# Input projection of a hybrid encoder layer: activations fetched six tiles ahead, inverse roots as powers on GpSimd, first weights in two halves

## The reference, cut to what matters

```python
def rmsnorm(x, w):
    xf = x.astype(jnp.float32)
    y = xf * lax.rsqrt(jnp.mean(xf * xf, axis=-1, keepdims=True) + EPS)
    return (y * w.astype(jnp.float32)).astype(x.dtype)

def hybrid_layer(x, ...):
    xn = rmsnorm(x, norm_mix_w)
    proj = jnp.einsum('btd,de->bte', xn, w_in)
    # q, k, v, forget gate of the attention heads; q/k/v, gates, z of the delta-rule heads
    ...
    h = x + jnp.einsum('bte,ed->btd', mix, w_o)
    # a second norm, up-projection, causal conv, SiLU gate, down-projection, final norm
```

## Time and profile before

| | us |
|---|---|
| median of three runs (4260.08 to 4277.38) | 4275.02 |
| the profiled execution | 4281.21 |
| its span | 4279.7 |
| TensorE busy in it | 3964.6 (93%) |
| VectorE, ScalarE, GpSimd busy | 1663.3, 1283.9, 367.2 |
| piece 0, from its first row product (20.85) to the first of piece 1 (171.10) | 150.25 |

### The profile page before, as it was taken

One profiled execution on the slowest core, in us unless ns is written; L12 is line 12 of the kernel. 1 busy time (PEld: TensorE's weight loads), 2 busy tenths in 40 slices (PEclk: granted clock), 3 DMA queues, 4 the chain that ended last, 5 costly groups with the idle time before them and its releaser, 6 DMA issues. The chain is left out here.

```text
span 4279.7 us, 56482 instructions
## 1 busy us (share of the span) xinstructions
PE 3964.6 (93%) x21471; PEld 3380.8 (79%) x21471; DVE 1663.3 (39%) x3428; ACT 1283.9 (30%) x2333; POOL 367.2 (9%) x346
## 2 busy tenths in 40 slices
PE   5799999799999999989997997999999999899996
PEld 4799999677777777768885446999999999678775
DVE  2100177555445455433331333444444444331222
ACT  6311222233333333321100332333333333231122
POOL 2000000111112111111100000000000000010222
PEclk8899999899999999997777998999999999999999
DMA  2222122411222111042232331111111111342221
GB/s 91 73 68 66 57 69 72 96 33 29 55 42 55 41 36 35 17 134 72 82 104 92 103 100 50 53 43 45 43 52 45 43 43 43 103 125 73 83 83 55
DMA packets 318288, 278.71 MB, mean 65 GB/s; under 512 B 128530, under 2 KB 267394, under 8 KB 318039
## 3 DMA queue, kind: packets, MB, share of 16 engines
q1 hardware_dynamic: 297999, 247.47, 19.8%
q0 software_dynamic: 4896, 17.83, 1.1%
q10 hardware_dynamic: 15228, 11.10, 0.9%
HBM read 190.70 MB, written 85.65 MB: 65 GB/s over the span
## 5 line engine op out<-in xcount | busy, mean ns | idle before, releaser
L2185 PE MATMUL bank<-hn_hi,up_w_parts 128*128 128x436 f32 (+1 forms) x3520 | 981.5, 360 | 10.2 <-DVE up_w_parts L2260 10.2
L2185 PEld LDWEIGHTS bank<-hn_hi,up_w_parts 128*128 128x128 f32 x3520 | 662.1, 188 | 41.9 <-issue 10.3
L2185 PE MATMUL bank<-hn_lo,up_w_parts 128*128 128x436 f32 (+1 forms) x1760 | 632.8, 360 | 0.0
L2185 PEld LDWEIGHTS bank<-hn_lo,up_w_parts 128*128 128x128 f32 x1760 | 331.4, 188 | 19.1
L301 PE MATMUL bank<-proj_wh,proj_xh 128*128 128x256 f32 (+1 forms) x1088 | 318.6, 293 | 2.0 <-DVE proj_wl L467 2.0
L301 PE MATMUL bank<-proj_wl,proj_xh 128*128 128x256 f32 (+1 forms) x1088 | 314.5, 289 | 0.0
L301 PE MATMUL bank<-proj_wh,proj_xl 128*128 128x256 f32 (+1 forms) x1088 | 314.1, 289 | 0.0
L2231 ACT COPY up_raw<-bank 128x436 f32<-128x436 f32 (+1 forms) x220 | 110.3, 502 | 642.2 <-PE bank L2185 612.1
L1365 PE MATMUL bank<-heads_p_pT,heads_p_v 128*65 128x512 f32 (+3 forms) x640 | 287.1, 530 | 10.3 <-issue 10.1
L2434 PE MATMUL bank<-down_w_hi,down_g_hi 128*128 (+1 forms) x748 | 238.1, 400 | 50.2 <-DVE down_g_lo L2529 42.8
L2529 DVE TENSOR_TENSOR down_g_lo<-down_g_raw,down_g_hi 128x256 fp32r<-128x256 f32 (+1 forms) x198 | 111.0, 561 | 389.2 <-ACT down_g_hi L2494 389.2
(11 more groups left out here) (390 smaller groups left out, 6977.1 us busy)
## 6 DMA issues: line engine op xcount, KB each, us to landing
up_w<-in_w_up_dram SPq DMA_DIRECT2D x44, 512.0 KB, 4.8
down_g_raw<-scratch_g SPq DMA_DIRECT2D x88, 256.0 KB, 2.6
scratch_g<-up_acc SPq DMA_DIRECT2D x88, 218.0 KB, 2.0
heads_s_k<-in_cache_fox_k_dram SPq DMA_DIRECT2D x8, 2048.0 KB, 9.4
heads_s_v<-in_cache_fox_v_dram SPq DMA_DIRECT2D x8, 2048.0 KB, 8.1
heads_d_qkvT<-scratch_gch SPq DMA_DIRECT2D x17, 768.0 KB
down_y<-in_w_down_dram SPq DMA_DIRECT2D x22, 512.0 KB, 3.6
scratch_gch<-proj_work SPq DMA_DIRECT2D x48, 218.0 KB, 1.9
```

The source lines that it names most:

```text
L2185: mm = pe.matmul(bank[:, pair(n) + e, 0:width], w_parts[:, a, part, e, k, :], x[:, k, cols], start=(k == 0 and m == 0), stop=(k == KD - 1 ...
```

## The change

- **Fetches of x** go six tiles ahead (`AHEAD`) into two new names, `raw_h` and `raw_l`, which lie on the same memory as `xh` and `xl` in places that are not filled yet: tiles 0 to 7 in a row of `xl` that belongs to later tokens, tiles 8 to 16 in the place in `xh` that the tile itself will fill, as 8 runs of 128 elements. A fetch waits for the square of tile t - 6. `normalise` reads from there and writes to `work`.
- **The inverse root** leaves ScalarE, which only squares now, one tile to four ahead of `row_out`. GpSimd computes (sum / D + eps) to the power -0.5 in two instructions, for tile 0 alone and then for two tiles at once (`inverse_root`). GpSimd's constants come behind the last of them.
- **The first weights** are fetched, scaled and split in two halves of the width, the second piece's fetch is written between the fetches of tiles 3 and 4, and `split_hi(1)` and `split_lo(1)` move to behind tiles 9 and 12. `sums` moves behind `split_lo(2)`.

```diff
+    with ExitStack() as lent:
+        whole, ph.stack = ph.stack, lent
+        raw_h, raw_l = (ph.sb(n, [P, KD, TOK]) for n in ("raw_h", "raw_l"))
+        ph.stack = whole
     xh, xl = (ph.sb(n, [P, KD, TOK], F32R) for n in ("xh", "xl"))
...
+    AHEAD = 6
+    groups = [(0,)] + [(t, t + 1) for t in range(1, NT, 2)]
...
+    def raw_x(t):
+
+        if t < KD:
+            return raw_l[:, t, KD * P:2 * KD * P].rearrange("p (k c) -> p k c", c=P)
+        return raw_h[:, :, t * P:(t + 1) * P]
...
             def load_x(t):
-                if t >= 2:
-                    sp.wait_ge(xn_turned, 2 * (t - 2) + 2)
+                if t >= AHEAD:
+                    sp.wait_ge(x_squared, t - AHEAD + 1)
...
             load_x(0)
...
-            load_w(0)
-            load_x(1)
+            for h in range(2):
+                load_first_w(h)
+            for t in range(1, 4):
+                load_x(t)
+            load_w(1)
+            for t in range(4, AHEAD):
+                load_x(t)
...
-            load_w(1)
             for p in range(NR):
                 for t in range(NT):
-                    if p == 0 and t + 2 < NT:
-                        load_x(t + 2)
+                    if p == 0 and t + AHEAD < NT:
+                        load_x(t + AHEAD)
...
         def _(act):
-            def norm_factor(t):
...
-                nc.scalar.activation(ln_ms[:, s:s + 1], ss[:, s:s + 1], ACT.Ln, scale=1.0 / D, bias=c["eps"][:]) \
...
-                nc.scalar.activation(rs[:, s:s + 1], ln_ms[:, s:s + 1], ACT.Exp, scale=-0.5).then_inc(rs_ready, 1)
+            def square(t):
+                act.wait_ge(x_loaded[t % AHEAD], 16 * (t // AHEAD) + 16)
+                if t >= 1:
+                    act.wait_ge(x_squared, t)
+                nc.scalar.activation(squares.rearrange("p (k c) -> p k c", c=P), raw_x(t), ACT.Square,
+                                     accum_out=ss[:, t:t + 1]).then_inc(x_squared, 1)
...
-            norm_factor(0)
-            norm_factor(1)
+            for t in range(3):
+                square(t)
+            for h in range(2):
+                first_hi(h)
             keep_hi(0)
-            split_hi(0)
+            square(3)
             keep_hi(1)
             for t in range(NT):
-                if t + 2 < NT:
-                    norm_factor(t + 2)
+                if t + 4 < NT:
+                    square(t + 4)
                 row_out(0, t)
                 if t + 2 < NT:
                     keep_hi(t + 2)
-                if t == 6:
+                if t == 9:
                     split_hi(1)
...
             normalise(0)
+            for h in range(2):
+                first_lo(h)
+            keep_lo(0)
             normalise(1)
-            keep_lo(0)
-            split_lo(0)
             keep_lo(1)
             for t in range(2, NT):
                 normalise(t)
                 keep_lo(t)
-                if t == 9:
+                if t == 12:
                     split_lo(1)
...
+            def inverse_root(g):
+                first, n = groups[g][0], len(groups[g])
+                cols = slice(first, first + n)
+                pool.wait_ge(x_squared, first + n)
+                nc.gpsimd.tensor_scalar(ss[:, cols], ss[:, cols], 1.0 / D, EPS, ALU.mult, ALU.add).then_inc(ms_ready, 1)
+                pool.wait_ge(ms_ready, g + 1)
+                nc.gpsimd.tensor_tensor(rs[:, cols], ss[:, cols], half[:, 0:n], ALU.pow).then_inc(rs_ready, 1)
...
-            scale_w(0)
+            first_scaled(0)
+            first_scaled(1)
+            for g in range(1, 5):
+                inverse_root(g)
             scale_w(1)
+            for g in range(5, len(groups)):
+                inverse_root(g)
             make_constants(nc, c, pool, step, later, upto)
```

More of the change, by code:

```diff
@@ L159, in project @@
     work = ph.sb("work", [P, 2 * D])
-    x = work[:].rearrange("p (a n) -> p a n", a=2)
+    xn = work[:].rearrange("p (a n) -> p a n", a=2)
+    AHEAD = 6
+    groups = [(0,)] + [(t, t + 1) for t in range(1, NT, 2)]
+    group_of = {t: g for g, ts in enumerate(groups) for t in ts}
     LR = H3 + TP + DB * (H3 + DS)
@@ L170, in project @@
     vec_rows, vecs = ph.sb("vec_rows", [NV, P]), ph.sb("vecs", [P, NV])
-    ss, ln_ms, rs = (ph.sb(n, [P, 2]) for n in ("ss", "ln_ms", "rs"))
+    ss, rs, half = ph.sb("ss", [P, NT]), ph.sb("rs", [P, NT]), ph.sb("half", [P, 2])
     hist = ph.sb("hist", [P, NCH, R])
@@ L181, in project @@
         "pool_step", "ident_ready", "consts_ready", "sums_done"))
-    x_loaded = [ph.sem(f"x_loaded{n}") for n in range(2)]
+    x_loaded = [ph.sem(f"x_loaded{n}") for n in range(AHEAD)]
+    w0_loaded = [ph.sem(f"w0_loaded{n}") for n in range(2)]
+    w0_scaled, w0_hi, w0_lo = ph.sem("w0_scaled"), ph.sem("w0_hi"), ph.sem("w0_lo")
     vec_loaded, small_loaded, tails_loaded, w_loaded = (ph.sem(n) for n in (
@@ L299, in row_products @@
                 for k in range(KD):
+                    if r == 0 and k % HB == 0:
+                        pe.wait_ge(w0_lo, k // HB + 1)
                     for m, (a, b) in enumerate(((xh, wh), (xh, wl), (xl, wh))):
@@ L344, in _, with first_hi @@
         def _(act):
[L345 to L356 removed]
+            def square(t):
[4 more added lines that the diff above has]
+                                     accum_out=ss[:, t:t + 1]).then_inc(x_squared, 1)
+            def first_hi(h):
+                act.wait_ge(w0_scaled, h + 1)
+                nc.scalar.copy(wh[:, 0, k_half(h), 0:halves], w[:, k_half(h), 0:halves]).then_inc(w0_hi, 1)
             def keep_hi(t):
@@ L567, in scale_w, with first_scaled @@
                 n = width(p)
-                pool.wait_ge(w_loaded, 16 * p + 16)
+                pool.wait_ge(w_loaded, 16 * p)
                 nc.gpsimd.tensor_tensor(w[:, :, 0:n], w[:, :, 0:n], spread(vecs[:, 0:KD].unsqueeze(2), [P, KD, n]),
                                         ALU.mult).then_inc(w_scaled, 1)
+            def first_scaled(h):
+                pool.wait_ge(w0_loaded[h], 16)
+                nc.gpsimd.tensor_tensor(w[:, k_half(h), 0:halves], w[:, k_half(h), 0:halves],
+                                        spread(vecs[:, k_half(h)].unsqueeze(2), [P, HB, halves]), ALU.mult) \
+                    .then_inc(w0_scaled, 1)
+            def inverse_root(g):
[5 more added lines that the diff above has]
+                nc.gpsimd.tensor_tensor(rs[:, cols], ss[:, cols], half[:, 0:n], ALU.pow).then_inc(rs_ready, 1)
             step = Step(pool, pool_step)
+            step(nc.gpsimd.memset(half[:], -0.5))
             step(nc.gpsimd.memset(c["eps"][:], EPS))
```

46 lines of the change are left out of this document (31 added, 15 removed).

## The result

The changed kernel took 4201.5 us (median of 4 runs, 4191.8 to 4204.0) against 4272.5 for the kernel before (4 runs): a ratio of 0.9834 with a 95% interval of 0.9807 to 0.9861, 71 us less and well over the 0.5% that can be told from no change. The forecast was 4198, in a range of 4183 to 4224. The profiled execution took 4200.2 us with a span of 4198.7; before it was 4281.2 and 4279.7, so 81.0 us of span are to be found.

What follows compares the result with a forecast made beforehand. Bound: piece 0's chain through ScalarE and the fetch, 8.8 us a tile, leaving TensorE idle or slow. 19.4 + 61.0 + 1.0 + 0.3 + 0.8 + 11.4 = 93.9 for 171.1, so 4275.0 - 77 = 4198 us; range 4183 to 4224.

Steps and rivals of the forecast that it cites:

- Parts 1 and 2: Piece 0: ScalarE loses 34 table loads of 1.28 us, leaving 2.7 a tile; GpSimd makes a root pair in 1.0.
- Rival 1: Hand-over chain between turnings sets piece 0's pace, 4.4 to 4.5 us a tile: 4209, or 4222 at worst; chance 0.20.
- Part 3: Fetches of x in 512-byte runs take 4.0 us, between 3.8 and 5.5, all hidden behind two tiles of work.
- Rival 4: Nine tiles' 512-byte fetches make it slower than before, eating the gain from 12.3 us each; 4309 at 16; chance 0.02.
- The pace: In piece 0 TensorE sets 3.69 us a tile at 2.4 GHz; the 3.4 us chain fits under by 0.3.
- rival 2: Small pauses keep TensorE at 1.2 GHz in piece 0, 6.7 us a tile: 4244 at worst, 4221 for half; chance 0.08.
- The 0.3 for tile 3's hand-over: A term of 0.3 us added to piece 0's sum for the hand-over at tile 3.
- Part 4: Start with halved first weights: first row product at 19.4 us in place of 20.85, between 18.5 and 22.
- The slow first product: At the start, the first row product begins at 1.2 GHz and costs 1 us more than 2.84.
- Part 5: Late in piece 0, tile 15's fetch stands behind weight piece 2: a new stop of 11.4 us, between 7 and 15.
- Rival 3: The new stop is short, as the fetch lands early or engines run further ahead: 8 us less, 4190; chance 0.15.
- The sum: Terms put piece 1's first row product at 93.9 us, where it was 171.1: 77 less, time 4198.

Runs made afterwards that it cites:

- fetches alone: Changed kernel with the inverse roots back on ScalarE as Ln and Exp behind each square, x still six tiles ahead: 4224.8 us, ratio 0.9881.
- roots alone: Changed kernel with x fetched two tiles ahead, waiting for the turning; roots on GpSimd tile by tile; second weights split where before: 4241.0 us, 0.9918.
- the doubled normalising: Changed kernel with every normalising instruction of piece 0 done twice on VectorE, same result: 4209.9 us in one run.
- split at the end: Changed kernel with second weights' split behind the last tile, third weights' fetch behind the store of tile 15, second scaling in four quarters: 4183.1 us, 0.9786.
- third weights behind tile 16: Changed kernel with the third weights' fetch moved behind the store of tile 10, so behind the fetch of tile 16: 4192.8 us, 0.9800.
- five tiles ahead: Changed kernel with x fetched five tiles ahead in place of six and third weights behind the store of tile 11: 4181.3 us in one run.

## Why the prediction was right

**The bound, and one link misread.** That ScalarE's square-to-eviction chain and a fetch lay on one ring was right. That "the fetch after next may start only once the turning is over" was wrong: the turning of tile t was long over when tile t + 2 was asked for (it began at 67.02 for the fetch at 75.55). The fetch stood behind the store of tile t - 1 in SyncE's list, and the store waited for the eviction that ScalarE had behind the square and both table loads of another tile. Ring: 4.18 from the square to the eviction, 0.4 to the store, 0.4 to the fetch, 5.0 to the next square, together the 9.92 us from the square at 70.61 to that at 80.53. That is a long one: nine of the fourteen distances are 8.6 to 8.9, with a fetch of 3.8 in place of 5.0 in most. Moving the fetch ahead of the store gave 28 us by itself. The misreading cost the forecast nothing, since the change removes that link as well; it made my numbers for the partial versions poor.

**Parts 1 and 2, ScalarE and the roots.** Right. The pair of roots took 1.0 to 1.2 us (taken: 1.0), of which the power 0.69 (line through the rows: 0.71). Rival 1 did not come: the roots are ready 1.0 to 3.1 us early, and no normalising took over 0.75 us but the two beside the scalings. Of the 34 table loads four, for tiles 0 and 1, lay ahead of piece 0 and not in it. The two parts give 47.6 (fetches alone) and 37.3 (roots alone) at the mark and 77.9 together, so neither does nearly everything, and they overlap by only 7.0, in part the halved first weights that both have: the fetches alone leave ScalarE as the bound at 5.40, the roots alone leave the ring at 6.8, and only both reach TensorE's 3.70.

**Part 3, the fetches.** Right: 4.1 to 4.8 us in runs of 512 bytes (taken 4.0, bounds 3.8 to 5.5), and hidden, even from five ahead. Tile 4, behind the second weights, came 2.1 us late, which the prediction didn't have and which cost nothing. Rival 4 fell (its 12.3 us should read 12.2).

**The pace.** 3.70 for 3.69. The cover that I worked out as 0.3 us is 0.4 by the doubled normalising, and the clock stayed up (1.00 from 22.55 to 66.28; rival 2 fell). The 0.3 for tile 3's hand-over did not come: its turning stands 3.69 behind tile 2's.

**Part 4, the start.** The first row product came at 18.75 for 19.4, since the last remainder of the first weights ended at 15.2 (12.86 + 2.36) and not at 15.7, and tile 1 was turned from 17.13 on. Being early was luck. The prediction had no wait of tile 1's square for its fetch, and that wait sets this start: in the three kernels with the same start (split at the end, third weights behind tile 16, five tiles ahead) the first row product came at 19.18, 19.80 and 20.06. The slow first product cost 3.80 - 2.84 = 0.96 (1.0). `normalise(0)` took 2.38 us beside the first scaling. The hold beside the second cost TensorE 41.84 - 37.36 - 3.70 = 0.78 (0.8), 0.63 of it idle.

**Part 5, the stop.** SyncE's fetch at 65.58 (66.4), the wait of the square 10.19 (some 10), TensorE's gaps 1.99 and 6.44 (2.5 and 6.7). By the distances of the turnings at 60.41, 66.28, 76.65 and 82.94, each less 3.70, the stop cost 2.17 + 6.67 + 2.59 = 11.4 us, and 11.4 was the forecast. With the third weights out of the way 9.2 came back from the turning of tile 2 on, beside 6.67 + 2.59 = 9.3; the mark shows 8.2, because that run started 1.0 later. Rival 3 fell, and its 8 us were there to be had only by another edit.

**The sum.** 93.20 for 93.9, from 171.10: 77.9 for 77. The start gave 0.65 of the 0.7 us by which 93.20 is early, and a start like that of the other three kernels would have put it at 94.2 to 94.7 (an estimate: 93.20 - 22.55 = 70.65 behind their turnings of tile 2). GpSimd's constants kept clear, as forecast: the scaling of the third weights was done at 101.0 (102), and TensorE is busy for all 48.30 us of piece 1. Another 3.1 us went behind the mark, which no term had and which the scatter there covers. The median of the runs fell by 74 against the one of the prediction, 71 against that of the runs beside it, both off the 77 by less than single runs scatter.

## What to carry to other kernels

A wait that the profile names "DMA" says that the data came late, not why: look at what stands ahead of the fetch in its queue's list, and whom *that* waits for. Here a store that waited for an eviction held every fetch, and one swapped place was worth 28 us. When a change removes the last wait of a ring, count which engine is next (5.40, 6.8 or 3.70 here) and look through every queue for the one transfer that now comes at a bad place; a piece of weights in front of two tiles of x cost some 9 us and moved for nothing. And before a mark in one trace is believed to a microsecond, look at how far the same start lies apart in traces that share it.

## What the runs showed of the hardware

The hold of VectorE and GpSimd on each other also reaches short instructions. The two-column power took 0.69 us at 23.32 and 36.99, but 1.69 at 12.96, beside the remainder of the first weights that VectorE had begun at 12.86; its first half took 1.22 us, to 14.08. The small instruction ahead of the power took 0.41 at 36.49, to 36.90, beside the normalising from 36.11 to 36.85, where it takes 0.20 undisturbed. The prediction had only the long GpSimd instruction as a row. The Trainium skill, "SBUF — State Buffer", "Who interferes with whom", has it that whichever starts first keeps the shared ports to its end; these rows agree, and so does the kernel that normalises twice, where the power at 32.26 took 1.20 beside the second normalising (32.16 to 32.91).

The other way round, a power that holds VectorE, is what the prediction set against its sum by the same rule. It did not show, and for so short an instruction the row is not what the rule would give: in the kernel with the split at the end the power began first, at 12.91, and ended at 13.61, and the remainder that VectorE began at 13.29 took its 1.22 us a half all the same, as it does where no power runs. All of this cost no time here, because each root had 1.0 us of cover or more.

The power's cost is close to linear in its columns: 0.58 us for one (at 7.84), 0.69 for two, with 1.04 and 1.69 for four and eight.
